# Mixer B, 16 attention heads in pairs: transposes two steps behind the scores, a third buffer of probabilities, weights rounded ahead of the exponentials, half of the scaling on POOL

## The reference, cut to what matters

```python
proj = h @ w_in + b_in                      # q: 1024 columns, k: 256, v: 256
s = einsum(q, keys of this and the block before) * 64 ** -0.5, masked to a window of 128
p = softmax(concatenate([s, sink]))[..., :-1]
o = einsum(p, v)
return o.reshape(B, T, 1024) @ w_out + b_out
```

## Time and profile before

| what | us |
|---|---|
| median of 3 runs | 1618.59 (1618.41 to 1620.3) |
| the profiled execution, its own time | 1617.96 |
| its span in the trace | 1616.2 |
| busy in the span: PE / DVE / ACT / POOL | 1518.0 / 1097.8 / 768.5 / 90.6 |
| mean granted TensorE clock, share of full | 0.973 |
| stage B, from its first weight product (799.1) to the first of F3 (918.1) | 119 |
| of this the loop over pairs, first `scores` (822.80) to the end of the last `outputs` (893.53) | 70.7 |

### The profile page before, as it was taken

How to read it: one execution, slowest core, us unless ns; L and a number is a source line. 1 busy time by engine, 2 the same in 40 slices (tenths; PEclk the granted TensorE clock), 3 DMA queues, 4 the chain that set the end, 5 groups by cost and what they waited for, 6 DMA issues and landing times.

```text
span 1616.2 us, 26076 instructions
## 1 busy us (share of the span) xinstructions
PE 1518.0 (94%) x10408; PEld 1355.4 (84%) x10408; DVE 1097.8 (68%) x1341; ACT 768.5 (48%) x1012; POOL 90.6 (6%) x84
## 2 busy tenths in 40 slices
PE   7999999788999999999977899999999979999997
PEld 6888899788888888888866888888988867878886
DVE  6877578664678767776566577856656665678764
ACT  6554368633544444544445454445254433454532
POOL 2000200100000010000100000003022010000001
PEclk9999999998999999999979999999999999999999
DMA  8554665310365556655631346366453322555551
GB/s 283 169 194 143 208 198 158 112 55 2 131 192 177 174 180 200 196 171 170 213 128 53 130 157 198 122 220 208 129 153 105 105 79 79 183 168 171 174 182 58
DMA packets 243967, 247.47 MB, mean 153 GB/s; under 512 B 4993, under 2 KB 242321, under 8 KB 243889
## 3 DMA queue, kind: packets, MB, share of 16 engines
q1 hardware_dynamic: 242112, 242.89, 47.0%
q0 software_dynamic: 1056, 2.30, 0.4%
q10 hardware_dynamic: 720, 1.17, 0.2%
HBM read 245.30 MB, written 1.05 MB: 152 GB/s over the span
## 4 chain that ended last, share of the span: by engine, by line
PE 78%; DVE 10%; ACT 7%; issue 3%; DMA 1%; POOL 0%; SPq 0%; ACTq 0%; DVEq 0%; POOLq 0%
PE ps L335 37%; PE ps L336 19%; ACT whi L299 4%; DVE wlo L305 3%; PE ps L339 2%; PE ps L340 2%; PE ps L341 2%; PE ps L1854 2%; PE ps L1855 2%; PE ps L1856 2%; PE ps L1119 1%; PE ps L1878 1%; PE ps L1866 1%; PE ps L2019 1%; PE ps L436 1%
## 5 line engine op out<-in xcount | busy, mean ns | idle before, releaser
L335 PE MATMUL ps<-u,whi 128*128 128x512 f32 x1744 | 617.2, 398 | 11.5 <-DVE u L405 11.5
L305 DVE TENSOR_TENSOR wlo<-raw,whi 128x2048 fp32r<-128x2048 f32 (+3 forms) x260 | 532.7, 2080 | 123.3 <-ACT whi L299 123.3
L336 PE MATMUL ps<-u,wlo 128*128 128x256 f32 x1744 | 493.3, 283 | 0.0
L299 ACT ACTIVATE whi<-raw 128x2048 fp32r<-128x2048 f32 (+3 forms) x260 | 438.0, 1721 | 56.6 <-PE ps L336 44.7
L335 PEld LDWEIGHTS ps<-u,whi 128*128 128x128 f32 x1744 | 330.1, 189 | 88.6 <-DVE u L405 12.8
L336 PEld LDWEIGHTS ps<-u,wlo 128*128 128x128 f32 x1744 | 332.0, 190 | 0.2
L335 PE MATMUL ps<-h,whi 128*128 128x512 f32 x880 | 308.1, 394 | 0.0
L336 PE MATMUL ps<-h,wlo 128*128 128x256 f32 x880 | 247.5, 281 | 0.0
L335 PEld LDWEIGHTS ps<-h,whi 128*128 128x128 f32 x880 | 165.4, 188 | 38.1
L336 PEld LDWEIGHTS ps<-h,wlo 128*128 128x128 f32 x880 | 166.1, 189 | 0.0
L339 PE MATMUL ps<-u,whi 128*128 128x256 f32 (+1 forms) x488 | 142.2, 291 | 5.4 <-DVE u L631 2.9
(11 more groups left out here) (363 smaller groups left out, 2102.9 us busy)
## 6 DMA issues: line engine op xcount, KB each, us to landing
raw<-in_ffn_w_gu SPq DMA_DIRECT2D x87, 1024.0 KB, 5.7
raw<-in_ffn_w_down SPq DMA_DIRECT2D x32, 768.0 KB, 5.4
raw<-in_w_in SPq DMA_DIRECT2D x22, 1024.0 KB, 5.3
raw<-in_ffn_w_down SPq DMA_DIRECT2D x32, 640.0 KB, 4.7
raw<-in_a_w_in SPq DMA_DIRECT2D x16, 1024.0 KB, 5.9
raw<-in_w_ffn_gate SPq DMA_DIRECT2D x11, 1024.0 KB, 5.4
raw<-in_w_ffn_up SPq DMA_DIRECT2D x11, 1024.0 KB, 6.3
raw<-in_b_w_in SPq DMA_DIRECT2D x6, 1024.0 KB, 7.2
```

Of the source, the lines that this page charges most:

```text
L299: nc.scalar.activation(whi[:, s, 0:n], raw[:, s, 0:n], ACT.Copy).then_inc(w_hi, 1)
L305: nc.vector.tensor_tensor(wlo[:, s, 0:n], raw[:, s, 0:n], whi[:, s, 0:n].bitcast(F32), ALU.subtract).then_inc(w_lo, 1)
L335: nc.tensor.matmul(o, whi[:, s, w], both, start=(first and k == 0), stop=False)
L336: ins = nc.tensor.matmul(o[:, 0], wlo[:, s, w], both[:, 0], start=False, stop=(last and k == nk - 1))
```

## The change

It moves, in stage B alone:

- PE: per step `q_block` or `out_part` comes first, then `scores(i)`, `outputs(i-3)`, `transposes(i-2)`; the loop has 11 steps, and `out_part` starts in step 7. The banks of the second and third input slot are swapped, and `q_block(0)` no longer waits for the first queries' eviction.
- ACT: slots are rounded before the exponentials, one every second step; the sink's exponential is taken from `nm` with the sink as bias, two small instructions a pair.
- DVE: `nm` is one instruction for a pair, against a negated sink `b_ns`; the sink's argument is gone; only the 256-wide parts of the probabilities are scaled.
- POOL: it makes `b_ns` and scales the 128-wide parts of both heads in one product a pair, in place. `transposes` waits for it too (semaphore `pp`).
- `b_p` has three buffers; `b_pt` moves to the scratch area `scr_at`.

```diff
+            b_p = place("b_p", [P, 3, 2, BS], at=h_at + 24576)
+            b_pt = place("b_pt", [P, 2, 2, BS], at=scr_at)
...
+            B_IN = (0, 5, 2)
...
 b_pool
             pool.wait_ge(sbn["tab"], 32)
+            nc.gpsimd.tensor_scalar(b_ns[:, :], b_sink[:, :], -1.0, None, ALU.mult).then_inc(sbn["pp"], 1)
+            for j in range(PAIRS):
+                pool.wait_ge(sbn["r"], 2 * j + 2)
+                part = b_p[:, j % 3, :, Q_PARTS[0]]
+                nc.gpsimd.tensor_tensor(part, part, b_r[:, 2 * j:2 * j + 2, 0].unsqueeze(2).broadcast_to([P, 2, P]),
+                                        ALU.mult).then_inc(sbn["pp"], 1)
 q_block
-                if i < 2:
-                    pe.wait_ge(sbn["in"], 3)
-                else:
+                if i >= 2:
                     pe.wait_ge(sbn["qe"], i - 1)
 transposes
                 pe.wait_ge(sbn["p"], i + 1)
+                pe.wait_ge(sbn["pp"], i + 2)
+                if i == 0:
+                    pe.wait_ge(sbn["in"], 3)
 b_pe, LAG = 2
-            for i in range(PAIRS + 2):
+            for i in range(PAIRS + LAG + 1):
+                if i < 6:
+                    q_block(i)
+                elif i == 7 or i == 8:
+                    if i == 7:
+                        pe.wait_ge(w_lo, MORE + gd + 1)
+                    pe.wait_ge(sbn["qe"], i - 2)
+                    out_part(0, [i - 7], range(0, 4))
+                elif i == 10:
+                    out_part(0, [0, 1], range(4, 6))
                 if i < PAIRS:
                     scores(i)
-                if i >= 2:
-                    outputs(i - 2)
-                if i < 6:
-                    q_block(i)
-                elif i < 8:
...
-                if 1 <= i <= PAIRS:
-                    transposes(i - 1)
+                if i > LAG:
+                    outputs(i - LAG - 1)
+                if LAG <= i < PAIRS + LAG:
+                    transposes(i - LAG)
 b_act
+                ahead.to(g0 + min(6 + i // 2, 10))
                 if i < PAIRS:
-                    act.wait_ge(sbn["nm"], 2 * i + 1)
-                    if i >= 2:
-                        act.wait_ge(sbn["pt"], i - 1)
+                    act.wait_ge(sbn["nm"], i + 1)
+                    if i >= 3:
+                        act.wait_ge(sbn["pt"], i - 2)
...
-                    nc.scalar.activation(b_es[:, pair], b_sd[:, pair], ACT.Exp).then_inc(sbn["ex"], 1)
-                ahead.to(g0 + min(6 + (i + 1) // 2 + (i == 0), 10))
+                        ins = nc.scalar.activation(b_es[:, h], b_nm[:, h], ACT.Exp, bias=b_sink[:, h:h + 1])
+                    ins.then_inc(sbn["ex"], 1)
 b_dve
-                    for h in (2 * i, 2 * i + 1):
-                        ins = nc.vector.tensor_scalar(b_nm[:, h], b_mx[:, h], b_sink[:, h:h + 1], -1.0, ALU.max, ALU.mult)
-                    ins.then_inc(sbn["nm"], 1)
-                    dve.wait_ge(sbn["nm"], 2 * i + 1)
-                    nc.vector.tensor_tensor(b_sd[:, pair], b_nm[:, pair], b_sink[:, pair].unsqueeze(2).broadcast_to([P, 2, 2]),
-                                            ALU.add).then_inc(sbn["nm"], 1)
+                    nc.vector.scalar_tensor_tensor(b_nm[:, pair], b_mx[:, pair], -1.0, b_ns[:, pair].unsqueeze(2).broadcast_to([P, 2, 2]),
+                                                   ALU.mult, ALU.min).then_inc(sbn["nm"], 1)
...
-                        for t in range(2):
-                            part = b_p[:, j % 2, e, Q_PARTS[t]]
-                            ins = nc.vector.tensor_scalar(part, part, b_r[:, 2 * j + e, t:t + 1], None, ALU.mult)
+                        part = b_p[:, j % 3, e, Q_PARTS[1]]
+                        ins = nc.vector.tensor_scalar(part, part, b_r[:, 2 * j + e, 1:2], None, ALU.mult)
...
+                ahead.to(g0 + min(6 + i // 2, 10))
```

More of the change, by code:

```diff
@@ L1567, in b_pe @@
             for m in range(3):
-                b0 = (0, 2, 5)[m]
+                b0 = B_IN[m]
                 slot_blocks(pe, g0 + m, [ps[:, b0 + b, 0:SEQ] for b in range(2)], (uhi, ulo), tok=tok,
@@ L1625, in b_act @@
                     with_bias(b_q[:, i + 1], b_tmp[:, (i - 1) // 2 % 2, (i - 1) % 2], w0 + i + 1).then_inc(sbn["bias"], 1)
[L1626 to L1628 removed]
+                if i > LAG:
+                    j = i - LAG - 1
+                    act.wait_ge(sbn["o"], j + 1)
+                    nc.scalar.activation(b_oh[:, j, tok], ps[:, 4 + 3 * (j % 2), 0:SEQ], ACT.Copy).then_inc(sbn["oh"], 1)
+                ahead.to(g0 + min(6 + i // 2, 10))
                 if i < PAIRS:
                     pair = slice(2 * i, 2 * i + 2)
[L1631 to L1633 removed]
+                    act.wait_ge(sbn["nm"], i + 1)
+                    if i >= 3:
+                        act.wait_ge(sbn["pt"], i - 2)
                     for e in range(2):
@@ L1636, in b_act @@
                         for t in range(2):
-                            nc.scalar.activation(b_p[:, i % 2, e, Q_PARTS[t]], b_s[:, i % 2, e, Q_PARTS[t]], ACT.Exp,
+                            nc.scalar.activation(b_p[:, i % 3, e, Q_PARTS[t]], b_s[:, i % 2, e, Q_PARTS[t]], ACT.Exp,
                                                  bias=b_nm[:, h, t:t + 1], accum_out=b_sum[:, h, t:t + 1])
-                    act.wait_ge(sbn["nm"], 2 * i + 2)
-                    nc.scalar.activation(b_es[:, pair], b_sd[:, pair], ACT.Exp).then_inc(sbn["ex"], 1)
-                ahead.to(g0 + min(6 + (i + 1) // 2 + (i == 0), 10))
[L1642 to L1646, removed]
+                        ins = nc.scalar.activation(b_es[:, h], b_nm[:, h], ACT.Exp, bias=b_sink[:, h:h + 1])
+                    ins.then_inc(sbn["ex"], 1)
+                if LAG <= i < PAIRS + LAG:
+                    j = i - LAG
+                    act.wait_ge(sbn["pt"], j + 1)
+                    if j >= 2:
+                        act.wait_ge(sbn["o"], j - 1)
+                    nc.scalar.activation(b_pt[:, j % 2], ps[:, 2:4, 0:BS], ACT.Copy).then_inc(sbn["ptc"], 1)
             out_act(act, "B", next_of("B"), 1, ahead)
@@ L1672, in b_dve @@
             mask2 = b_mask[:, :].unsqueeze(1).broadcast_to([P, 2, BS])
-            for i in range(PAIRS + 3):
+            dve.wait_ge(sbn["pp"], 1)
+            for i in range(PAIRS + LAG + 1):
                 if 1 <= i <= 6:
```

21 lines of the change are left out of this document (7 added, 14 removed).

## The result

The changed kernel takes 1600.65 us (median of 4 runs, 1600.23 to 1602.83) against 1619.34 before (median of 4): a ratio of 0.9887, 95% interval 0.987 to 0.9904. It is 18.7 us faster; forecast were 1600.0, between 1595 and 1608.5.

The account below looks back on a forecast made before the run. A ring of waits, not a full engine, bounds the loop over pairs. The walk's gain of 21.2 us less 1.8 for clock and 0.8 for POOL is 18.6: 1599.4, median 0.6 higher, so 1600.0, range 1595 to 1608.5.

Parts of the forecast that it names:

- What bounds it: Stage B's loop over pairs, 70.7 us: no engine is full, a ring of waits sets it.
- The walk: Loop timed step by step at full clock: last outputs start at 871.5 instead of 892.73, a gain of 21.2 us.
- The sum: Gain of 21.2 less 1.8 and 0.8 is 18.6 us, so 1600.0; chance 0.50.
- The 1.8 for the clock: Deduction for one low-clock stretch on PE in the loop: two thirds of 2.6 us.
- The 0.8 for POOL: Deduction for DVE instructions slowed beside POOL's product in the loop, between nothing and 3.2 us.
- ACT's second exponential: Second small sink exponential on ACT: 0.1 us more a pair, 1.97 instead of 1.87.
- The ring of b_pt: From the seventh scores, b_pt, outputs, b_oh, slot and exponentials bind: 5.7 us with a slot, 3.9 without or DVE's step.
- DVE's relief: DVE's pair falls from about 4.6 to 3.95 us: about 0.38 from scalings, 0.25 from nm and sink argument.
- POOL beside DVE: POOL's product stretches DVE instructions beside it, as a wlo by 0.4 us; only some pairs contended.
- Rival 1: POOL's product slows DVE in every pair, 0.4 x 8 = 3.2 us: gain 16.2, 1602.4; chance 0.20.
- Behind the loop: The list after the loop is the same; F3 starts 24.6 us after it, as before, at no cost.
- Rivals 2 to 4: Low clock stays from seventh scores, 1607.6, 0.22; DVE's work binds, no change, 0.04; POOL's product far dearer, 1625, 0.04.

Follow-up runs that it names:

- e5: The kernel before with one part of the change alone: slots rounded ahead of the exponentials, one every second step; 1604.6 us.
- e7: The changed kernel with the sink's argument made on DVE again and one sink exponential a pair on ACT instead of two; 1600.46 us.
- e11: The changed kernel with all scalings on DVE, two buffers of probabilities and one sink exponential a pair; 1600.17 us.
- e12: The kernel of e11 with the last slot (step 8) rounded after the loop; 1594.45 us.
- e1: The changed kernel with all four scalings of the probabilities back on DVE, POOL making only the negated sink; 1600.6 us.
- e2: The changed kernel with slots rounded after the exponentials again, by the old rule (two in step 0); 1614.14 us.
- e6: The changed kernel with slots by the new rule (one every second step) but rounded after the exponentials; 1616.62 us.
- e3: The changed kernel with transposes one step behind the scores instead of two (LAG = 1, ten steps); 1617.07 us.
- e9: The changed kernel with slots rounded in steps 0, 1, 3, 5 and after the loop, instead of 0, 2, 4, 6, 8; 1600.39 us.

## Why the prediction was right, point by point

- **What bounds it.** Right: a ring of waits in the loop, not an engine. The long stall of DVE behind the two slots of step 0 was named, and third scores at 8.9 us after the first came at 9.0. What the text did not see is how much of the gain the place and rule of the slots bring alone: e5 shows 13.9 of 18.4 us, over all five slots and not only the first.
- **The walk.** Its milestones hold within 0.1 us up to the fourth scores and within 0.9 up to the seventh; the eighth scores came 2.1 us late and the last outputs 2.8. Of these 2.8 us, 1.2 are there at the last outputs but one (46.9 us against 45.65 in the walk), and 0.8 of them already at the seventh scores, before the clock falls: the walk's waits for b_pt were a few tenths too short from the fifth scores on. The other 1.6 are the last step, which the walk gives 3.05 us and which takes 4.61 at the low clock; e7 runs it in 3.03 at the high one. The fall after the wait of 2.57 us (the transposes at 857.94 take 1.24) lies under ACT's slot and exponentials, and cost the outputs behind it nothing where e11 and e12 let it be compared.
- **The sum.** It comes out, 48.7 + 1.8 + 0.8 = 51.3 against 51.5, but in part by luck. The 1.8 for the clock was right in size (1.6), though it was counted for one low stretch and there were two, of which one cost nothing that the traces show. The 0.8 for POOL meets the 1.2 us by which the walk was too short, and those are not shown to be POOL's: 0.2 to 0.4 of them go with ACT's second exponential (e7 and e11 are that much earlier at the last outputs but one), and the rest was not taken apart.
- **The ring of b_pt.** Right: PE waits there 8.9 us in seven waits, the longest 2.6, as the walk had it, and in the loop nowhere else over 1.1.
- **DVE's relief.** Wrong in size. Of the 0.65 us a pair, the 0.38 for the two scalings came to nothing (0.99 against 0.92, more than before); nm with the sink argument gave what was said, 0.16 for the new instruction and no argument.
- **ACT's second exponential.** Taken at 0.1 us a pair, it costs 0.26: two at 0.18 in place of one at 0.10.
- **POOL beside DVE.** Rival 1's mechanism is there in every pair, and at rival 1's size: 0.46 us x 8 = 3.7 of DVE's time, where rival 1 had 3.2 and the forecast 0.8. But it hits the scalings and not wlo, all five of which take 2.27 to 2.29 us. By the walk's own count at most 1.2 of these 3.7 us reached the last outputs but one, so most of it lay off the path, as the forecast said against rival 1. e1 can't size that share, since the halves that POOL took over had been worth about 0.4 us a pair themselves.
- **Behind the loop.** Right: 32.0 us against 31.9.
- **Rivals 2 to 4.** The low clock lasted for two stretches of 3 to 4 us (858.0 to 861.7 and 871.9 to 875.3 by the matmuls' times), not for the rest of the loop. Transposes never waited for POOL, whose product took 0.61 us.

The cause of the gain is shown by e5, e2, e6 and e3: the slots' place, and PE work between scores and transposes. The parts don't add up: early slots without the rest give 13.9, the rest without early slots 2.3 to 5.1, and early slots with the block first but one step of distance 0.2. What stays open is how the remaining 4.5 us, from e5 to the changed kernel, split over PE's order, its second step of distance and the early `q_block(0)`, and how much of the gain is the clock's: 0.83 became 0.93 in the loop, and no experiment held it fixed.

## What to carry to other kernels

Two engines that hand work to each other through in-order lists should do filler work (here, rounding a slot) ahead of the instruction that waits for the partner, not behind it, where the partner's next piece is queued behind that filler: here the place alone was worth 16.1 us (e6). This holds as long as there is a wait to fill; in e9 a slot in another step delayed the fourth scores by 1.4 us. A pipeline lag and the order within a step are one decision; ask how much work of the waiting engine lies between producer and consumer, and count it in us. Before work is moved to GpSimd to relieve VectorE, look at what VectorE's instructions beside it cost then.

## What the runs showed that I had not expected

- Two DVE scalings of 128x256 beside a POOL product of 128x256 take 1.07 us; alone 0.35 each. One of the two takes it all (0.81, the other 0.34). A wlo of 128x2048 was stretched by 0.4 us elsewhere: the loss is about as large for an instruction six times shorter.
- The place where the granted clock falls differs between executions of nearly the same list: after a wait of 2.56 us it fell in e12 and not in e11, and after one of 2.18 us it fell in the changed kernel and not in e7.
- Stage A's granted clock differs between executions too, and what follows starts earlier or later by it. From 200 to 300 us the windows of the changed kernel and of e7 read:

```profile
200.00:300.00 100.00, 94.47 (x747) 93.22 (x746) 79.60 (x116) 73.18 (x146) 5.96 (x6) 0.95 0.57 170
```

```profile
200.00:300.00 100.00, 93.81 (x780) 92.22 (x778) 80.94 (x117) 76.73 (x152) 5.95 (x6) 1.00 0.56 165
```

e7's B began 6.9 us earlier than the changed kernel's, more than most of the edits tried here are worth.
